# Bias strip and lambda products moved ahead of the first unit of a decoder trunk kernel

## The chip, the cores and the metric

The kernel runs on one core of one Trainium2 chip. The metric is the device time of one execution in microseconds (us); lower is better. The median of three runs stands for the kernel.

## The reference

The reference is a decoder trunk of two layers (sequence 256, width 2048). Only the first layer's mixer matters here:

```python
def parallel_mixer(h, w_in, w_out, rel_bias, lq1, lk1, lq2, lk2, subln, layer_idx):
    proj = jnp.einsum('bsd,de->bse', h, w_in)
    ...
    lam = (jnp.exp(jnp.sum(lq1 * lk1)) - jnp.exp(jnp.sum(lq2 * lk2)) + lam_init)
    a_out = diff_attention(aq, ak, av, rel_bias, lam, subln, lam_init)
    r_out = retention(rq, rk, rv, rg)
    mixed = jnp.concatenate([a_out, r_out], axis=-1)
    return jnp.einsum('bse,ed->bsd', mixed, w_out)
```

In `diff_attention` every softmax map gets a bias `rel_bias[bucket(distance)]`, and the second map of each head is subtracted with the weight `lam`. The rest of the trunk (a pooling mixer, two gated MLPs with a width-3 convolution, norms) is computed around it and is not touched.

## The kernel before

All weight matrices pass through the core in units of 512 x 512. SyncE (SP) loads a unit into one of four `raw` slots. ScalarE (ACT) rounds each of its four 128 x 512 tiles into `hi` (float32r), VectorE (DVE) writes the remainder `lo = raw - hi`, and TensorE (PE) multiplies with `hi` and `lo`. A pair of semaphores, `hi_done` and `lo_done`, counts the tiles, and `w_used` gives the single `hi`/`lo` buffer of each tile back.

The input projection has 56 units (14 groups of 4). The first four are done by `first_unit` (L640 to L655): per tile two products with `hi`, two with `lo`, and two with the low part of the activations (L645, L649, L653), each behind its own wait. These four units are loaded tile by tile, in the opening of the kernel. From unit 4 on, `token_unit` does the same in another order (L666, L671).

Two small things are prepared beside this stream. The *bias strip* is one product of `relb` (the relative bias, 32 x 8, and a row of ones) and `onehot` (33 x 384); ACT copies it out, writes it to memory and reads it back as a shifted pattern `bias`. *Lambda* begins with `lamp = lamv * lamv` on DVE (L1665), then a product with a matrix of ones on PE (L772), then an exponential on ACT (L1051) and two small steps on DVE. `strip_and_lambda` (L766 to L772) issues both products on PE. It is called behind unit 6 and behind the product `sum_squares` (L679) that adds up the squares of the first norm. The first reader of both results on PE is `scores` behind unit 12.

The data come by `CONSTS`, five small loads that SP issues behind its load for unit 4 (L474): `relb`, `onehot`, `lamv`, the identity and `sub`. All five count into one semaphore `c_in`; PE waits for it in `strip_and_lambda`, DVE behind unit 5 (L1664).

PE's program begins with a wait for the ones matrix (`setup`) and eight products of ones with ones into an unused bank (L776, `WARM_UP`); then the units come in the order of the text. Each float32 product stands as two passes in the trace. DVE's program begins with three memsets and a cast (L1609 to L1613) and goes on with `lo` of unit 0. GpSimd's program waits for the end of the kernel, where it multiplies a part of the last norm (L2013); it has no other work. Each engine runs its own list in order; nothing but the semaphores ties them.

Of the kernel before, what the change touches and what calls it, by code (L numbers as in the profile page):

```python
# [23 lines left out]
ALU = mybir.AluOpType  # L24
# [7 lines left out]
LAM_INIT = 0.8 - 0.6 * math.exp(-0.3 * 0)  # L32
POOL_WINDOWS = (2, 4, 8, 16)
RAW_SLOTS = 4
WARM_UP = 8
KT = 4


def trunk_kernel(nc, xT, rel_bias, norm_g, w_in, w_out, lam, subln, pool_w, pool_scale,
# [12 lines left out]
    NB = rel_bias.shape[0]  # L52
# [83 lines left out]
    with ctx:  # L136
        mixer = ExitStack()

        def sb(name, shape, dt=F32, stack=ctx):
            return stack.enter_context(nc.sbuf_tensor(name, shape, dt))  # L140
# [17 lines left out]
        ident = sb("ident", [P, P])  # L158

        with mixer:  # L160
# [19 lines left out]
            onehot = sb("onehot", [NB + 1, SPAN], stack=mixer)  # L180
            relb = sb("relb", [NB + 1, BD], stack=mixer)
            strip = sc[0:BD, 0, :]
            lamv = sb("lamv", [P, 4], stack=mixer)
            lamp = sb("lamp", [P, 4], stack=mixer)
            sub = sb("sub", [P, 2], stack=mixer)
# [3 lines left out]
            rden = sb("rden", [P, 4], stack=mixer)  # L189
        gate = bias  # L190
        am_blocks = mt[:, :, :].rearrange("p t s -> p (t s)")[:, 0:384]
        CONSTS = [(relb[0:NB, :], rel_bias), (onehot[:, :], bucket_onehot), (lamv[:, :], lam),
                  (ident[:, :], ident_in), (sub[:, :], subln)]
        TABLES = [(cos[:, :], rot_cos), (sin[:, :], rot_sin), (dec[:, :, :], decay), (pscale[:, :], pool_scale),
                  (pool_m[:, :, :], pool_matrix), (cw[:, :, :, :], conv)]
        N_CONST = len(CONSTS)
        N_TABLE = len(TABLES)
# [7 lines left out]
        def sem(name):  # L205
            return ctx.enter_context(nc.semaphore(name))
# [3 lines left out]
        w_tile = [sem(f"w_tile{i}") for i in range(12)]  # L210
        g_in = sem("g_in")
        c_in = sem("c_in")
        table_in = sem("table_in")
        raw_full = [sem(f"raw_full{i}") for i in range(RAW_SLOTS)]
        hi_done = sem("hi_done")
# [18 lines left out]
        lam_prod = sem("lam_prod")  # L234
# [109 lines left out]
        def acc_banks(i):  # L344

            return ps[:, 2 * (i % 2):2 * (i % 2) + 2, :]
# [35 lines left out]
        def _(sp):  # L382
# [55 lines left out]
            for n in range(U_OUT):  # L438
# [33 lines left out]
                if n == 4:  # L472
                    for dst, src in CONSTS:
                        sp.dma_start(dst, src).then_inc(c_in, 16)  # L474
# [66 lines left out]
        def _(pe):  # L541
# [133 lines left out]
            def sum_squares(n, bank):  # L675

                pe.wait_ge(sq_added, SQ_BASE[n + 1])
                if n != 2:
                    mm = pe.matmul(ps[:, bank, 0:S], ones[:, :], sqacc[:, 0, :], start=True, stop=True,  # L679
                                   skip_group_check=True)  # L680
                if n == 2:

                    for t in range(2):
                        mm = pe.matmul(ps[:, bank, S + t:S + t + 1], sqacc[:, 0, t * P:(t + 1) * P], ones[:, 0:1],
                                       start=t == 0, stop=True, skip_group_check=True)
                mm.then_inc(norm_sum, 1)
# [39 lines left out]
            def head_squares(n):  # L726

                if n == 0:
                    pe.wait_ge(ones_rounded, 1)
                pe.wait_ge(squares_lo, n + 1)  # L730
                if n:
                    pe.wait_ge(ssq_kept, n)
                pe.matmul(ps[:, 6, 0:S], ones_r[:, :], sq_hi[:, :], start=True, stop=False, skip_group_check=True)
                pe.matmul(ps[:, 6, 0:S], ones_r[:, :], sq_lo[:, :], start=False, stop=True,
                          skip_group_check=True).then_inc(ssq_mm, 1)
# [29 lines left out]

            def strip_and_lambda():  # L766

                pe.wait_ge(c_in, 16 * N_CONST)
                pe.wait_ge(setup, 3)
                pe.matmul(ps[0:BD, 4, 0:SPAN], relb[:, :], onehot[:, :], start=True, stop=True).then_inc(strip_mm, 1)  # L770
                pe.wait_ge(lam_prod, 1)
                pe.matmul(ps[:, 5, 0:2], ones[:, :], lamp[:, 0:2], start=True, stop=True).then_inc(lam_sum, 1)  # L772

            pe.wait_ge(setup, 1)
            for _ in range(WARM_UP):
                pe.matmul(ps[:, 7, 0:P], ones[:, :], ones[:, :], start=True, stop=True, skip_group_check=True)  # L776

            for n in range(U_OUT):
                G, j = divmod(n, 4)
                if n in ACC_AT:  # L780
                    i = ACC_AT[n]
                    if i >= 2 and ACCS[i - 2][0] in QUAD_GROUPS:
                        pe.wait_ge(rows_turned, QUAD_GROUPS.index(ACCS[i - 2][0]) + 1)
                    elif i == 2:
                        pe.wait_ge(first_turned, 1)
                    elif i > 2:
                        pe.wait_ge(evacuated, ACC_OUT[i - 2])

                def beside(kt, n=n):
                    for head, unit_n in enumerate(SQUARES_AT):  # L790
                        if (n, kt) == (unit_n, 1):
                            head_squares(head)

                if GROUPS[G][1] in "tq":
                    token_unit(n, acc_banks(i), j == 0, j == 3, j, beside)
                elif GROUPS[G][1] == "f":
                    half_unit(n, acc_banks(i), j % 2 == 0, j % 2 == 1, j % 2, beside)
                else:
                    first_unit(n, acc_banks(i))
                if n == 6:  # L800
                    sum_squares(0, 7)
                    strip_and_lambda()
                for a, at in enumerate(ATTN_START):
                    if n == at:
                        scores(a)
                    if n == at + 4:
                        attend(a)
                for r, at in enumerate(RET_START):
                    if n == at:
                        ret_scores(r)  # L810
                    if n == at + 1:
                        retain(r)
# [527 lines left out]
        def _(ve):  # L1340
# [270 lines left out]
            ve.memset(relb[NB:NB + 1, :], 1.0).then_inc(setup, 1)  # L1611
            ve.wait_ge(setup, 1)
            ve.tensor_copy(ones_r[:, :], ones[:, :]).then_inc(ones_rounded, 1)  # L1613
            for n in range(4):
                for kt in range(KT):
                    w_lo(n, 0, n, [kt])
                    h_lo_group(0, n, 0, [kt])
# [39 lines left out]
            for n in range(4, U_OUT):  # L1657
                w_lo(n, 0, n % 4, between=beside_lo(n))
                if n == 4:
                    turn_first_rows()  # L1660
                if n == 6:
                    fold_squares(0)
                if n == 5:
                    ve.wait_ge(c_in, 16 * N_CONST)  # L1664
                    ve.tensor_tensor(lamp[:, 0:2], lamv[:, 0:2], lamv[:, 2:4], ALU.mult).then_inc(lam_prod, 1)  # L1665
                    ve.tensor_scalar(sub[:, :], sub[:, :], 1.0 - LAM_INIT, None, ALU.mult).then_inc(setup, 1)
                if n == 46:
                    scale_quads(10)
                if n - 1 in ACC_END and n > 4:
                    if (n - 1) // 4 in QUAD_GROUPS:  # L1670
                        turn_rows((n - 1) // 4)
                    else:
                        take_out(ACC_END[n - 1])
                if n == 9:

                    ve.wait_ge(lam_exp, 1)
                    ve.tensor_tensor(lamv[:, 1:2], lamp[:, 3:4], lamp[:, 2:3], ALU.subtract).then_inc(lam_done, 1)
                    ve.wait_ge(lam_done, 1)
                    ve.tensor_scalar(lamv[:, 0:1], lamv[:, 1:2], -LAM_INIT, None, ALU.add).then_inc(lam_done, 1)
                for a, at in enumerate(ATTN_START):  # L1680
                    if n == at + 1:
                        softmax_front(a)
                    if n == at + 2:
                        softmax_back(a)
                        turn_maps(a)
                    if n == at + 5:
                        fold_head(a)
                for r, at in enumerate(RET_START):
                    if n == at + 1:
                        decay_scores(r)  # L1690
                    if n == at + 2:
                        fold_head(4 + r)
# [314 lines left out]
        @block.gpsimd  # L2007
        def _(pool_e):
            g_ = nc.gpsimd
            pool_e.wait_ge(weighted, 12)  # L2010
            for t in range(2):
                pool_e.wait_ge(rstd_copied, t + 1)
                g_.tensor_tensor(x[:, 8:12, token[t]], x[:, 8:12, token[t]],  # L2013
                                 rstd[:, token[t]].unsqueeze(1).to_broadcast([P, 4, P]), ALU.mult).then_inc(out_pool, 1)
# [82 lines left out]
```

## Time and profile before

| what | before |
|---|---|
| median of three runs | 1904.09 us (1903.6 to 1904.84) |
| the profiled execution | 1903.54 us |
| its span, first to last instruction | 1901.8 us |
| PE busy | 1893.7 us |
| DVE busy | 1415.2 us |
| ACT busy | 1065.3 us |
| GpSimd busy | 2.8 us |

The profiled execution took 1903.54 us, of which 1901.8 us are its span and 1.74 us lie around it; it is 0.55 us under the median. Times in the rows below count from the start of the span. A timeline row gives the start, the duration, the engine, the line and the operation with its tiles, and in brackets for how long the engine sat idle before it and what ended this. An engine name with a q (SPq, ACTq, POOLq) is the queue of that engine's sequencer, on which DMAs and other instructions without arithmetic stand; PEld is the loading of the stationary matrix.

### The profile page before, as it was taken

What the parts mean: (1) busy time and instruction counts of PE and PEld (TensorE: products, weight loads), DVE (VectorE), ACT (ScalarE), POOL (GpSimd) and SP (SyncE); (2) the same over time, 40 slices, a digit from 0 to 9 for tenths busy, and PEclk for the clock granted to TensorE, in tenths of its full rate; (3) what the DMA queues carried; (4) which work ended last, traced back from release to release, by engine and by line L of the source; (5) the groups of instructions that cost most, each with busy time, mean ns of one, the idle gap of its engine ahead of it and who ended that gap; (6) DMA issues with size and microseconds to landing.
All of it is one profiled execution on the core that took longest, in us unless ns stands there. A gap on an engine that the chain in (4) does not pass through costs nothing.

```text
span 1901.8 us, 26641 instructions
## 1 busy us (share of the span) xinstructions
PE 1893.7 (100%) x8570; PEld 1574.7 (83%) x8570; DVE 1415.2 (74%) x2329; ACT 1065.3 (56%) x1796; POOL 2.8 (0%) x6
## 2 busy tenths in 40 slices
PE   9999999999999999999999999999999999999998
PEld 7888888888888888888888888888888888888887
DVE  7767977777777777777766678777777777766665
ACT  7555545556555655556554556565555655555544
POOL 0000000000000000000000000000000000000000
PEclk9999999999999999999999999999999999999999
DMA  9876666666887777776665555677777777755653
GB/s 317 276 230 212 204 213 198 221 206 212 246 242 234 241 238 245 246 242 218 210 214 199 195 183 191 218 242 236 244 246 244 238 230 249 245 180 197 218 199 111
DMA packets 234384, 424.58 MB, mean 223 GB/s; under 512 B 14115, under 2 KB 54988, under 8 KB 234316
## 3 DMA queue, kind: packets, MB, share of 16 engines
q1 hardware_dynamic: 201484, 376.83, 61.6%
q10 hardware_dynamic: 32832, 46.86, 8.3%
q8 instruction: 41, 0.67, 0.1%
q14 instruction: 27, 0.22, 0.0%
HBM read 390.86 MB, written 31.21 MB: 222 GB/s over the span
## 4 chain that ended last, share of the span: by engine, by line
PE 100%; ACT 0%; DVE 0%; issue 0%
PE ps L666 61%; PE ps L671 30%; PE ps L552 2%; PE ps L556 1%; PE ps L630 1%; PE ps L645 0%; PE ps L649 0%; PE ps L634 0%; PE ps L653 0%; PE ps L595 0%; PE ps L597 0%; PE ps L596 0%; PE ps L776 0%; PE ps L841 0%; PE ps L843 0%; PE ps L747 0%
## 5 line engine op out<-in xcount | busy, mean ns | idle before, releaser
L915 ACT ACTIVATE hi<-raw 128x512 fp32r<-128x512 f32 x1336 | 831.9, 630 | 758.2 <-PE ps L671 710.9
L1345 DVE TENSOR_TENSOR lo<-raw,hi 128x512 fp32r<-128x512 f32 x1352 | 910.2, 689 | 449.2 <-ACT hi L915 437.1
L666 PE MATMUL ps<-hi,h 128*128 128x512 f32 x3648 | 977.7, 390 | 0.0
L666 PEld LDWEIGHTS ps<-hi,h 128*128 128x128 f32 x3648 | 682.7, 188 | 140.7
L671 PE MATMUL ps<-lo,h 128*128 128x512 f32 x1824 | 561.5, 389 | 0.0
L671 PEld LDWEIGHTS ps<-lo,h 128*128 128x128 f32 x1824 | 342.3, 188 | 71.5
L666 PE MATMUL ps<-hi,act 128*128 128x512 f32 x1296 | 346.4, 389 | 0.0
L666 PEld LDWEIGHTS ps<-hi,act 128*128 128x128 f32 x1296 | 243.2, 188 | 50.5
L671 PE MATMUL ps<-lo,act 128*128 128x512 f32 x648 | 199.5, 389 | 0.0
L671 PEld LDWEIGHTS ps<-lo,act 128*128 128x128 f32 x648 | 121.6, 188 | 25.2
L1120 ACT ACTIVATE yg<-u,cw 128x256 f32<-128x256 f32 x88 | 52.1, 592 | 18.8 <-DVE u L1774 18.8
L1120 ACT ACTIVATE yv<-u,cw 128x256 f32<-128x256 f32 x88 | 52.0, 591 | 14.8 <-DVE u L1774 14.8
L1774 DVE TENSOR_TENSOR u<-sqacc,rstd 128x512 f32<-128x512 f32 x84 | 54.1, 685 | 1.9 <-DMA sqacc<-turned_rows 1.9
L1763 DVE STREAM_TRANSPOSE sqt<-ps 128x1024 f32<-128x1024 f32 x42 | 52.2, 1243 | 0.0
L1809 DVE STREAM_TRANSPOSE u<-ps 32x256 f32<-32x256 f32 x96 | 42.8, 446 | 2.9
L552 PE MATMUL ps<-mixed,hi 128*128 128x512 f32 x128 | 43.9, 394 | 0.0
L1790 DVE SCALAR_TENSOR_TENSOR yg<-u,cw,yg 128x254 f32<-128x254 f32 x88 | 38.2, 477 | 0.0
L1782 DVE SCALAR_TENSOR_TENSOR yv<-u,cw,yv 128x255 f32<-128x255 f32 x88 | 36.6, 479 | 0.0
L1782 DVE SCALAR_TENSOR_TENSOR yg<-u,cw,yg 128x255 f32<-128x255 f32 x88 | 36.6, 479 | 0.0
L1790 DVE SCALAR_TENSOR_TENSOR yv<-u,cw,yv 128x254 f32<-128x254 f32 x88 | 36.5, 478 | 0.0
L666 PE MATMUL ps<-hi,mixed 128*128 128x512 f32 x128 | 34.2, 389 | 0.0
L556 PE MATMUL ps<-mixed,lo 128*128 128x256 f32 x128 | 34.2, 277 | 0.0
(208 smaller groups left out, 869.0 us busy)
## 6 DMA issues: line engine op xcount, KB each, us to landing
raw<-in_w_up SPq DMA_DIRECT2D x176, 1024.0 KB, 5.7
raw<-in_w_down SPq DMA_DIRECT2D x88, 1024.0 KB, 5.1
raw<-in_w_in SPq DMA_DIRECT2D x52, 1024.0 KB, 5.6
turned_rows<-sqt ACTq DMA_DIRECT2D x42, 512.0 KB, 5.9
sqacc<-turned_rows ACTq DMA_DIRECT2D x168, 128.0 KB, 6.0
raw<-in_w_out SPq DMA_DIRECT2D x16, 1024.0 KB, 6.0
raw<-in_w_in SPq DMA_DIRECT2D x16, 256.0 KB, 5.5
row_store<-sqt SPq DMA_DIRECT2D x8, 512.0 KB, 3.0
```

The source lines that it names most:

```text
L552: pe.matmul(ps[:, bank + m, :], hi[:, kt, m * P:(m + 1) * P], mv, start=first and kt == 0, stop=False, skip_group_check=True)
L556: return pe.matmul(ps[:, bank + m, S:2 * S], lo[:, kt, m * P:(m + 1) * P], mv[:, 0:S], start=False, stop=last and kt == KT - 1, skip_group ...
L666: pe.matmul(acc[:, t, :], xt, hi[:, kt, :], start=first and kt == 0 and half == 0, stop=False, skip_group_check=True)
L671: mm = pe.matmul(acc[:, t, :], xh, lo[:, kt, :], start=False, stop=last and kt == KT - 1, skip_group_check=True)
L915: a_.activation(out[:, kt, :], raw[:, slot, kt, :], ACT.Copy).then_inc(hi_done, 1)
L1120: a_.activation(y[:, m, :], u[:, m, :], ACT.Identity, scale=cw[:, l, bass.ds(t, 1), 2], bias=cw[:, l, bass.ds(t, 1), 3]).then_inc(y0, 1)
L1345: ve.tensor_tensor(halves[1][:, kt, :], raw[:, slot, kt, :], halves[0][:, kt, :].bitcast(F32), ALU.subtract).then_inc(lo_done, 1)
L1763: ve.transpose(turned_u.rearrange("p (q k s) -> p q k s", q=4, k=8), rows).then_inc(evacuated, 1)
L1774: scaled = ve.tensor_tensor(out, quads, r, ALU.mult)
L1782: ve.scalar_tensor_tensor(y[:, m, 1:S], u[:, m, 0:S - 1], cw[:, l, bass.ds(t, 1), 1], y[:, m, 1:S], ALU.mult, ALU.add).then_inc(y1, 1)
L1790: ve.scalar_tensor_tensor(y[:, m, 2:S], u[:, m, 0:S - 2], cw[:, l, bass.ds(t, 1), 0], y[:, m, 2:S], ALU.mult, ALU.add).then_inc(y2, 1)
L1809: ve.transpose(cols, rows).then_inc(x_turned, 1)
```

## The change

Three of the five small loads (`onehot`, `relb`, `lamv`) leave SP's list and stand first in GpSimd's, with a semaphore `early_in` of their own. DVE's product for lambda moves from behind unit 5 to ahead of `lo` of unit 0, behind a wait for `early_in`. The two products of `strip_and_lambda` move on PE from behind unit 6 to ahead of unit 0, behind a wait for `early_in`, and two of the eight products of ones are dropped.

```diff
-WARM_UP = 8
+WARM_UP = 6
...
-        CONSTS = [(relb[0:NB, :], rel_bias), (onehot[:, :], bucket_onehot), (lamv[:, :], lam),
-                  (ident[:, :], ident_in), (sub[:, :], subln)]
+        EARLY = [(onehot[:, :], bucket_onehot), (relb[0:NB, :], rel_bias), (lamv[:, :], lam)]
+        CONSTS = [(ident[:, :], ident_in), (sub[:, :], subln)]
...
+        early_in = sem("early_in")
...
             def strip_and_lambda():
-                pe.wait_ge(c_in, 16 * N_CONST)
+                pe.wait_ge(early_in, 16 * len(EARLY))
...
                 pe.matmul(ps[:, 7, 0:P], ones[:, :], ones[:, :], start=True, stop=True, skip_group_check=True)
+            strip_and_lambda()
...
                 if n == 6:
                     sum_squares(0, 7)
-                    strip_and_lambda()
...
             ve.tensor_copy(ones_r[:, :], ones[:, :]).then_inc(ones_rounded, 1)
+            ve.wait_ge(early_in, 16 * len(EARLY))
+            ve.tensor_tensor(lamp[:, 0:2], lamv[:, 0:2], lamv[:, 2:4], ALU.mult).then_inc(lam_prod, 1)
...
                 if n == 5:
                     ve.wait_ge(c_in, 16 * N_CONST)
-                    ve.tensor_tensor(lamp[:, 0:2], lamv[:, 0:2], lamv[:, 2:4], ALU.mult).then_inc(lam_prod, 1)
...
             g_ = nc.gpsimd
+            for dst, src in EARLY:
+                g_.dma_start(dst, src).then_inc(early_in, 16)
             pool_e.wait_ge(weighted, 12)
```

## Rows read from the trace of the kernel before

**Rows 1.** The page: busy time of each engine, and the chain that ended last.

```profile
PE 1893.7 (100%) x8570; PEld 1574.7 (83%) x8570; DVE 1415.2 (74%) x2329; ACT 1065.3 (56%) x1796; POOL 2.8 (0%) x6
...
PE 100%; ACT 0%; DVE 0%; issue 0%
```

**Rows 2.** Waits of PE over the whole span: total, times, longest.

```profile
PE ps L610 <- DVE rms L1980: 1.2, 1, 1.2
PE ps L776 <- DVE eps L1610: 1.1, 1, 1.1
```

**Rows 3.** Timeline, opening, PE and its weight loads.

```profile
1.06 3.78 PE L776 MATMUL ps<-ones 128*128 128x128 f32 x16 [1.06 <-DVE eps L1610]
...
4.93 0.46 PEld L645 LDWEIGHTS ps<-hi,h 128*128 128x128 f32 x2 [0.38 <-issue]
4.96 0.86 PE L645 MATMUL ps<-hi,h 128*128 128x512 f32 x2
...
7.16 0.30 PEld L649 LDWEIGHTS ps<-lo,h 128*128 128x128 f32 x2 [0.38 <-DVE lo L1345]
...
8.54 0.31 PEld L649 LDWEIGHTS ps<-lo,h 128*128 128x128 f32 x2 [0.15 <-DVE lo L1345]
```

**Rows 4.** Timeline, end of unit 3 and start of unit 4, PE alone.

```profile
24.57 0.62 PE L645 MATMUL ps<-hi,h 128*128 128x512 f32 x2
...
25.93 0.62 PE L645 MATMUL ps<-hi,h 128*128 128x512 f32 x2
...
27.29 1.07 PE L666 MATMUL ps<-hi,h 128*128 128x512 f32 x4
```

**Rows 5.** Chain that ended last, 40 to 48 us: start, us of the chain, what.

```profile
42.41 0.91 PE ps L666 x4
43.32 0.45 PE ps L671 x2
43.77 0.43 PE ps L679 x2
44.20 0.74 PE ps L770 x2
44.94 0.31 PE ps L772 x2
45.25 1.03 PE ps L666 x4
46.29 0.46 PE ps L671 x2
```

**Rows 6.** Timeline, opening, DMA issues, DVE and ACT.

```profile
0.75 0.43 ACTq L1005 DMA_DIRECT2D gains<-in_norm_g  x1
...
1.18 0.23 DVE L1613 CAST ones_r<-ones 128x128 fp32r<-128x128 f32 x1
...
1.21 0.44 ACTq L1006 DMA_DIRECT2D x<-in_xT  x1
...
1.69 1.28 ACT L1009 ACT_TABLE_LOAD   x1 [1.69 <-PEq L2087]
...
4.31 0.91 ACT L921 ACTIVATE h<-x,gains 128x256 fp32r<-128x256 f32 x2
4.41 0.69 DVE L1345 TENSOR_TENSOR lo<-raw,hi 128x512 fp32r<-128x512 f32 x1 [3.00 <-ACT hi L1018]
...
9.17 0.63 ACT L1018 ACTIVATE hi<-raw 128x512 fp32r<-128x512 f32 x1
...
11.90 0.69 DVE L1345 TENSOR_TENSOR lo<-raw,hi 128x512 fp32r<-128x512 f32 x1
```

**Rows 7.** Issues of the small loads on SP's queue (one line), and the next.

```profile
13.52 1.32 SPq L474 DMA_DIRECT2D relb<-in_rel_bias  x1
14.89 0.41 SPq L474 DMA_DIRECT2D onehot<-in_bucket_onehot  x1
15.34 0.36 SPq L474 DMA_DIRECT2D lamv<-in_lam  x1
...
16.69 0.43 SPq L387 DMA_DIRECT2D raw<-in_w_in  x1
```

**Rows 8.** DMA issues of 0 to 10 us: KB each, median us to landing.

```profile
x<-in_xT SPq DMA_DIRECT2D x7, 128.0 KB, 4.4
x<-in_xT SPq DMA_DIRECT2D x1, 512.0 KB, 5.9
x<-in_xT ACTq DMA_DIRECT2D x1, 128.0 KB, 3.2
gains<-in_norm_g ACTq DMA_DIRECT2D x1, 40.0 KB, 3.2
```

**Rows 9.** Lines 776, 719 and 645 by operation: ns min/median/max, first and last start.

```profile
L776 PE MATMUL ps<-ones x16: 421/421/581, 1.1 to 4.4; 128*128 128x128 f32 x16
...
L719 PE MATMUL ps<-amT,v x16: 270/274/275, 101.0 to 192.3; 128*128 128x128 f32 x16
...
L645 PE MATMUL ps<-hi,h x32: 387/389/632, 5.0 to 26.2; 128*128 128x512 f32 x32
```

**Rows 10.** Busy time by stretch: PE, PEld, DVE, ACT, POOL, PEclk (granted clock), DMA share, GB/s.

```profile
4.00:5.00 1.00, 0.88 (x5) 0.62 (x4) 0.59 (x1) 1.00 (x3) 0.00 (x0) 1.00 0.98 310
...
10.00:30.00 20.00, 20.00 (x89) 16.53 (x89) 16.30 (x30) 14.94 (x28) 0.00 (x0) 1.00 1.06 376
```

**Rows 11.** GpSimd's line 2013 by operation: ns min/median/max, first and last start.

```profile
L2013 POOLq MODIFY_POOL_CONFIG  x2: 11/11/11, 0.8 to 0.8; - x2
L2013 POOL TENSOR_TENSOR x<-x,rstd x2: 1267/1277/1287, 1888.0 to 1895.5; 128x512 f32<-128x512 f32 x2
```

**Rows 12.** DVE's product for lambda, from the instructions of tile lamp.

```profile
L1665 DVE TENSOR_TENSOR lamp<-lamv x1: 154/154/154, 34.7 to 34.7; 128x2 f32<-128x2 f32 x1
```

## The prediction

> **What bounds the kernel now.** I read the page first: PE is busy for 1893.7 of 1901.8 us, the chain that ended last is PE from end to end, and no other engine is over 1415.2 us [rows 1]. Then PE's waits: over the whole span there are only two that the profile counts, 1.1 us before the first product of ones and 1.2 us in the last norm [rows 2]. Between them PE goes from one product to the next. So time is won or lost in two ways only: PE gets fewer products (or faster ones), or its first unit starts earlier or later. What DVE, ACT and the weight loads do matters as far as it reaches the start of PE's stream. That the DMA engines are full from 10 to 30 us (share 1.06) costs PE nothing, for it is busy for all 20.00 us there [rows 10].
>
> The opening needs the timeline. PE runs the products of ones from 1.06 to 4.84 us, and unit 0 starts at 4.96 [rows 3], when ACT has `hi` and, from 4.31 us on, the first `h` [rows 6]. The first steps lose a little more: two waits for `lo`, 0.38 and 0.15 us [rows 3], and a slow first product (below). From there a tile takes 1.36 us (25.93 - 24.57) and unit 4 starts at 27.29 [rows 4]. Counted back over 16 tiles, 27.29 - 16 x 1.36 = 5.53 us: the stream runs as if it had started at 5.53 at its steady pace. This is the mark that the changed kernel has to meet.
>
> **The change part by part.** *Products behind unit 6.* In the chain the strip takes 0.74 us, lambda 0.31, and the four products behind them 1.03 instead of 0.91, for the stream restarts: 0.74 + 0.31 + 0.12 = 1.17 us [rows 5]. They go from there, and since nothing but PE is late behind them, all 1.17 us come off the end.
>
> *Two products of ones fewer.* Six take 6/8 of 3.78 = 2.83 us and end at 3.89 instead of 4.84 [rows 3]. This gains nothing by itself, since the data of unit 0 are there only at about 4.8 to 4.9 us [rows 6]. It makes room for 0.95 us.
>
> *Products ahead of unit 0.* They cost the same 1.17 us, but only from the time E at which all three early loads have landed. DVE's product for lambda (0.154 us, [rows 12]) runs beside the strip on PE. So the steady start moves to E + 1.17, and against before the balance is (E + 1.17 - 5.53) - 1.17 = E - 5.53: with PE at one pace, the change wins when the loads land before 5.53 us and loses when they land later. Everything hangs on E.
>
> *E.* The trace of before shows no DMA on GpSimd's queue, so I bound it. From below by ACT's queue, a second queue in the same moments: issues at 0.75 and 1.21, so 0.46 us apart [rows 6], each landing in 3.2 us [rows 8]. Three of them would land by 0.75 + 2 x 0.46 + 3.2 = 4.87 us. From above by the slowest issue of the same loads, `relb` on SP's queue with 1.37 us to the next (14.89 - 13.52, [rows 7]), and SP's landing of 4.4 us [rows 8]: 0.75 + 2 x 1.37 + 4.4 = 7.89 us. I take 5.6 us, a quarter of the way, because ACT's queue is the nearer row: the same microsecond and small loads beside SP's stream. The balance is then +0.1 us, between -0.7 and +2.4.
>
> The Trainium skill, "DMA: Bandwidth & Descriptors", section "Anatomy of one DMA — SWDGE (gpsimd) path", gives a DMA issued by GpSimd a fixed 2.0 us and its bytes at 436 GB/s; if three followed each other wholly, an estimate from that page would be 6.9 us for E and the balance +1.4. It speaks against the change; no run here shows the pace of that queue.
>
> *The clock.* The granted clock reads 1.00, the upper level (2.4 GHz), in the stretches of the opening [rows 10], but the durations say otherwise: a pass of 128 columns lasts 421 ns among the products of ones and 274 ns later, and the first pass of unit 0 lasts 632 ns against 389 [rows 9]. So PE runs at the lower level (1.2 GHz) from 1.06 to about 5.3 us, 4.3 us of unbroken work, and at the upper one from there. In the changed kernel PE stands idle from 3.89 to E. The strip and lambda may then run wholly at the lower level, and their 1.05 us of passes take at most 1.05 us more. I take somewhat over half of it, +0.6.
>
> *What DVE's wait holds up.* Behind it stand `lo` of unit 0 and all later ones; before, that first `lo` starts at 4.41 [rows 6]. With E = 5.6 it ends at about 5.6 + 0.15 + 0.69 = 6.45, still ahead of PE's need at about 7. ACT needs PE's first release for unit 1 at 9.17 and SP needs DVE's only from unit 4 on; with PE later by some 1.2 us both have slack. Nothing added.
>
> *Three loads off SP's queue.* Their issues go from 13.52 to 15.70 [rows 7]. The load of unit 5 stands behind them and can be issued about 2.2 us before 16.69: it waits only for `lo` of unit 1, which is done at about 12.6 [rows 6]. Its issue is earlier; PE has no wait there, so the gain is nothing. The 0.154 us taken out behind unit 5 on DVE are nothing either, since DVE waits for ACT.
>
> *The sum.* -1.17 + (5.6 + 1.17 - 5.53) + 0.6 = +0.7 us against the profiled execution, 1903.54 + 0.7 = 1904.2. That execution is 0.55 us under the median of 1904.09, so in terms of the median 1904.8. Own range of this case: -0.7 to 2.4 + 1.05 = +3.5, or 1903.4 to 1907.6.
>
> **The rivals.** *Hidden whole.* If the loads land by 3.8 us, the two products take the room of the dropped ones, unit 0 starts at 4.96 as before, and the kernel is 1.17 us faster: 1902.9. For it: a single early load can land by 0.75 + 3.2 = 3.95. Against it: there are three on one queue.
>
> *The clock starts again.* If the idle time makes the rise count anew from E, the first 4.3 us of work from there run at half pace and lose 2.2 us instead of 0.6: +0.1 + 2.2 = +2.3, 1906.4. For it: the rise came after 4.3 us of unbroken work in before. Against it: the pause is only 1.7 us.
>
> *The loads stand behind something on GpSimd (the other side).* GpSimd's queue carries two instructions MODIFY_POOL_CONFIG at 0.8 us that belong to line 2013, a multiplication that runs at 1888.0 [rows 11]. So they have been placed ahead of that line's waits, right where the early loads will stand, and what they start is not shown: 11 ns each on the queue. If they stand ahead of the loads and hold them, E moves by that time. The nearest row of an engine taking in tables is ACT's, 1.28 us [rows 6]; twice this gives E = 5.6 + 2.6 = 8.2, with 2.2 us for the clock a balance of +4.9: 1909.0. From E = 7.2 with the slow clock, or 9.3 without it, the loss passes 3.8 us. Against it: the pair belongs to a later line and may well stay behind the loads. The Trainium skill, "GPSIMD Engine Reference", section "Instruction dispatch", states that the first call to a freshly loaded kernel costs some 6 us more; by an estimate from that page E is 11.6 and the time about 1912. No row here shows such a load.
>
> **How the numbers follow.** Forecast 0.53, hidden whole 0.08, clock again 0.15, loads held 0.22, and 0.02 for a gain that no row shows. 0.2% of the kernel is 3.8 us, about what a measurement can tell from no change. The forecast, hidden whole and clock again all lie inside that, and so does 0.04 of the loads held: same 0.80. Slower is the rest of the loads held, 0.18; faster 0.02, since the products removed are worth 1.17 us at most. The range runs from 1902.9 (hidden whole) to 1909.0 (loads held by the nearest row) and leaves out the worse part of that rival, some 0.12.
>
> **What would show it.** In the changed trace: no L770 and L772 near 44 us, and 1.17 us between `sum_squares` and the next unit gone; six products of ones ending at 3.9; the start of the strip on PE, which is E, at 5 to 8 us; unit 4 starting E - 5.53 + 1.17 us (and the clock's part) later than 27.29; the first passes of unit 0 at 632 or at 389 ns. If the issue of the three loads on GpSimd starts well after 0.8 us, or the strip after 9, the loads were held and the forecast is wrong. If unit 0 starts by 5.0, all was hidden. A new wait of PE between 27 and 1890 us would speak against the whole way of counting.

## The result and the profile after

| what | before | after |
|---|---|---|
| median of 22 runs each | 1904.05 us (1903.6 to 1904.99) | 1907.26 us (1905.82 to 1909.44) |
| ratio to before | | 1.0016 (95% interval 1.0010 to 1.0022) |
| the profiled execution | 1903.54 us | 1909.44 us |
| its span | 1901.8 us | 1907.6 us |
| PE busy | 1893.7 us | 1896.1 us |

The change makes the kernel 3.2 us slower, 0.16%. That is inside the 0.2% called "same" in the prediction, and the interval is clear of no change. The runs of after lie further apart (3.6 us) than those of before (1.4 us), and the profiled execution is the slowest of them, so its 5.8 us of extra span are more than the 3.2 us of the medians.

The chain that ended last, in its first 16 us, tells the new opening (start, us of the chain, what):

```profile
1.27 0.71 POOL onehot L2013
1.99 0.51 POOL relb L2013
2.50 3.94 DMA lamv<-in_lam
6.44 0.04 issue
6.48 1.45 PE ps L771 x2
7.93 0.52 PE ps L773 x2
8.44 1.06 PE ps L646 x2
9.50 0.85 PE ps L650 x2
...
13.77 0.63 PE ps L646 x2
14.40 0.46 PE ps L650 x2
```

Before, this chain was PE alone. Now it begins on GpSimd: three issues, one behind the other, then the landing of the last load, and only then PE. The two lines L771 and L773 are the strip and lambda. Together they take 1.97 us here; behind unit 6 they took 1.05 [rows 5]. The passes of unit 0 take 0.85 us a pair and, from about 14 us on, 0.46. Unit 4 starts at 32.85 us (timeline, PE alone):

```profile
32.85 1.07 PE L667 MATMUL ps<-hi,h 128*128 128x512 f32 x4
```

The queue of GpSimd in the timeline, and the landings of its loads in the DMA issues of 0 to 12 us (KB, us to landing):

```profile
1.27 0.71 POOL L2013 DMA_DIRECT2D onehot<-in_bucket_onehot  x1 [0.82 <-POOLq L2091]
1.98 0.53 POOL L2013 DMA_DIRECT2D relb<-in_rel_bias  x1
2.50 0.57 POOL L2013 DMA_DIRECT2D lamv<-in_lam  x1
```

```profile
onehot<-in_bucket_onehot POOLq DMA_DIRECT2D x1, 49.5 KB, 3.7
relb<-in_rel_bias POOLq DMA_DIRECT2D x1, 1.0 KB, 3.5
lamv<-in_lam POOLq DMA_DIRECT2D x1, 2.0 KB, 3.9
```

So E, the time of the last landing, is 2.50 + 3.94 = 6.44 us. PE's waits and, by operation, lines 771, 773 and 646 (ns min/median/max, first and last start) answer to [rows 2, 9]:

```profile
PE ps L771 <- DMA lamv<-in_lam: 2.5, 1, 2.5
PE ps L611 <- DVE rms L1982: 1.2, 1, 1.2
PE ps L672 <- DVE lo L1346: 1.1, 1, 1.1
PE ps L777 <- DVE eps L1611: 1.1, 1, 1.1
```

```profile
L771 PE MATMUL ps<-onehot,relb x2: 806/825/844, 6.5 to 7.1; 33*8 33x384 f32 x2
L773 PE MATMUL ps<-lamp,ones x2: 352/362/372, 7.9 to 8.1; 128*128 128x2 f32 x2
...
L646 PE MATMUL ps<-hi,h x32: 389/389/774, 8.3 to 31.7; 128*128 128x512 f32 x32
```

PE waits 2.5 us for the loads, and what follows runs at the lower level of its clock (1.2 GHz): the first passes of unit 0 last up to 774 ns, against 389 later. The granted clock reads 1.00 there, so this is a reading of the durations; the run with later loads below shows passes of the same length where the granted clock reads 0.50.

Behind unit 6, the chain of 46 to 54 us shows what was won; the lines stand where [rows 5] stood:

```profile
49.33 0.43 PE ps L680 x2
49.76 0.93 PE ps L667 x4
50.69 0.46 PE ps L672 x2
```

From `sum_squares` on, the chain reaches the next L672 in 1.36 us in place of 2.52 (46.29 - 43.77): 1.16 us less.

The sum of the profiled execution: unit 4 starts at 32.85 us in place of 27.29 [rows 4], 5.56 us later; 1.16 come back behind unit 6; and the third wait above, near 1153 us, takes 1.49 us from one product to the next in place of 0.23, where DVE had sat 2.5 us waiting for a transfer that landed late. 5.56 - 1.16 + 1.26 = 5.7 of the 5.8 us. I do not count that last wait to the change: it stands in no profile of the experiments below in which both products are ahead of unit 0, and a shorter one for the same transfer (1.67 us on DVE, 0.26 us on PE) stands in the run with lambda alone moved. Why that transfer was late in this execution is not known.

### The profile page after: what moved, and what is told of

It is laid out like the page before. It is cut to its first block, busy times and chain, and to the rows that moved or that the text cites. A ratio compares the mean times of both kernels' runs of the same rounds, so it can differ in the third digit from the quotient of the medians.

```text
span 1907.6 us, 26633 instructions
## 1 busy us (share of the span) xinstructions
PE 1896.1 (99%) x8566; PEld 1576.1 (83%) x8566; DVE 1415.0 (74%) x2329; ACT 1063.9 (56%) x1796; POOL 4.5 (0%) x9
## 4 chain that ended last, share of the span: by engine, by line
PE 99%; DVE 0%; DMA 0%; issue 0%; ACT 0%; POOL 0%; DVEq 0%; POOLq 0%
PE ps L667 60%; PE ps L672 30%; PE ps L553 2%; PE ps L557 1%; PE ps L631 1%; PE ps L646 0%; PE ps L654 0%; PE ps L650 0%; PE ps L635 0%; PE ps L596 0%; PE ps L598 0%; PE ps L597 0%; DMA lamv<-in_lam 0%; PE ps L842 0%; PE ps L844 0%; PE ps L748 0%
## 5 line engine op out<-in xcount | busy, mean ns | idle before, releaser
L672 PE MATMUL ps<-lo,h 128*128 128x512 f32 x1824 | 561.7, 389 | 1.1 <-DVE lo L1346 1.1
L672 PEld LDWEIGHTS ps<-lo,h 128*128 128x128 f32 x1824 | 342.3, 188 | 72.9 <-DVE lo L1346 1.5
L672 PE MATMUL ps<-lo,act 128*128 128x512 f32 x648 | 199.4, 389 | 0.0
L672 PEld LDWEIGHTS ps<-lo,act 128*128 128x128 f32 x648 | 121.6, 188 | 25.3
```

The source lines that it names most:

```text
L672: mm = pe.matmul(acc[:, t, :], xh, lo[:, kt, :], start=False, stop=last and kt == KT - 1, skip_group_check=True)
```

## The experiments

The theory: with PE at one pace the change costs E - 5.53, so 6.44 - 5.53 = 0.9 us; the other 2.3 us come from the clock, which rises late because PE pauses from 4.00 to 6.48 us. The rivals: the pause is innocent, and the loads, GpSimd's queue, DVE's wait or the place of the products cost the time. "Before" is 1904.05 us for the first four and 1903.81 us for the last four, which were measured on another occasion. Eleven runs each.

**No pause.** The changed kernel with more products of ones:

```diff
-WARM_UP = 6
+WARM_UP = 14
```

> The changed kernel with 14 products of ones in place of 6, so that PE has work until the early loads land. Theory (late loads plus a clock that is not raised because PE pauses): the loads land at 6.4 to 6.5 us as in the changed kernel's trace, the clock rises near 5.3 us as before the change, and only E - 5.53 = about 0.9 us is left: 1905.0 us (1904.6 to 1905.4). Rival (the pause is innocent, the loss of 3.2 us comes from the loads, GpSimd's queue or the held DVE): 1907.3 us or more, for none of that is changed.

1904.79 us (1904.02 to 1906.08), ratio 1.0003 (0.9994 to 1.0012): 0.74 us over before, which by the interval could be nothing, and 2.47 under the changed kernel with 6. PE in its timeline:

```profile
1.07 5.79 PE L777 MATMUL ps<-ones 128*128 128x128 f32 x28 [1.07 <-DVE eps L1611]
6.79 0.81 PE L771 MATMUL ps<-onehot,relb 33*8 33x384 f32 x2
7.52 0.38 PE L773 MATMUL ps<-lamp,ones 128*128 128x2 f32 x2
7.77 0.72 PE L646 MATMUL ps<-hi,h 128*128 128x512 f32 x2
...
29.67 1.07 PE L667 MATMUL ps<-hi,h 128*128 128x512 f32 x4
```

The same loads, the same held DVE, the same order; only the pause is gone, and the strip takes 0.81 us in place of 1.45. The strip starts at 6.79 behind the last product of ones, a little after E. By the balance unit 4 should start at 27.29 + 6.79 + 1.17 - 5.53 = 29.72 us; it starts at 29.67. This execution (1905.64) is 0.85 us above the median: 0.9 us of its extra span come far behind the opening, about half of that at one wait for ACT near 1245 us.

**The pause alone.** The kernel before with fewer products of ones:

```diff
-WARM_UP = 8
+WARM_UP = 3
```

> The kernel before with 3 products of ones in place of 8 and nothing else, so that PE pauses from about 2.5 us to unit 0 at 4.96, as long as it pauses in the changed kernel (2.5 us). Theory: the clock rises later, unit 0 runs its first tiles at the lower level, and the time goes up by 1 to 4 us, 1906.3 us as the middle, with a wider spread from run to run than before (0.7 us). Rival (a pause is innocent): 1904.05 us, spread as before.

1905.88 us (1904.62 to 1908.78), ratio 1.0010 (1.0001 to 1.0019): 1.83 us slower with five products less. Its profiled execution, with 1904.79 us, is one of the lower ones:

```profile
1.06 1.65 PE L776 MATMUL ps<-ones 128*128 128x128 f32 x6 [1.06 <-DVE eps L1610]
5.12 1.19 PE L645 MATMUL ps<-hi,h 128*128 128x512 f32 x2 [2.40 <-ACT h L921]
6.11 1.05 PE L649 MATMUL ps<-lo,h 128*128 128x512 f32 x2
6.96 1.05 PE L653 MATMUL ps<-hi,h 128*128 128x512 f32 x2
7.81 0.90 PE L645 MATMUL ps<-hi,h 128*128 128x512 f32 x2
8.55 0.62 PE L649 MATMUL ps<-lo,h 128*128 128x512 f32 x2
```

Unit 0 starts 0.16 us later than before and stays at the lower level until about 8.4 us instead of 5.3. A pause of PE costs by itself about what the changed kernel lost beyond E, though the interval of the 1.83 us runs from 0.2 to 3.6. The wider spread is not shown: the 4.2 us come from one run, the other ten lie within 2.2 us, like the 33 runs of before that belong to them.

**The loads alone.** The kernel before, with the loads on GpSimd and all their users in the old places:

```diff
-        CONSTS = [(relb[0:NB, :], rel_bias), (onehot[:, :], bucket_onehot), (lamv[:, :], lam),
-                  (ident[:, :], ident_in), (sub[:, :], subln)]
+        EARLY = [(onehot[:, :], bucket_onehot), (relb[0:NB, :], rel_bias), (lamv[:, :], lam)]
+        CONSTS = [(ident[:, :], ident_in), (sub[:, :], subln)]
...
+            for dst, src in EARLY:
+                g_.dma_start(dst, src).then_inc(early_in, 16)
```

> The kernel before with the three loads issued by GpSimd at its start; both products and DVE's product stay behind units 6 and 5, with 8 products of ones. Theory: the loads are hidden, 1904.05 us (1903.8 to 1904.4), and the load of unit 5 is issued about 2 us earlier without any use. Rival (GpSimd's queue or the loads themselves disturb the opening or the end): 1905 to 1907.3 us.

1903.95 us (1903.27 to 1905.21), ratio 1.0000 (0.9991 to 1.0009). GpSimd's queue and the loads cost nothing that can be measured, and that three issues leave SP's queue gains nothing. The load of unit 5 is issued at 15.56 us, 1.1 us earlier than before [rows 7] and not 2.

**The products behind unit 0.** The changed kernel with 8 products of ones, and:

```diff
-            strip_and_lambda()
...
+                if n == 0:
+                    strip_and_lambda()
```

DVE's product moves behind its own work of unit 0 in the same way.

> The changed kernel with 8 products of ones, the two products behind unit 0 in place of ahead of it, and DVE's product behind its work of unit 0. By then (about 11 us) the loads have landed and the clock is up. Theory: PE's stream is full, so the products cost the same 1.17 us there as behind unit 6: 1904.05 us (1903.8 to 1904.5). Rival (taking them away from unit 6 is itself worth something, or being early costs something besides the wait): a difference of 1 us or more either way.

1904.08 us (1903.4 to 1905.32), ratio 1.0000 (0.9991 to 1.0009). PE in its timeline:

```profile
10.85 0.81 PE L771 MATMUL ps<-onehot,relb 33*8 33x384 f32 x2
...
28.25 1.07 PE L667 MATMUL ps<-hi,h 128*128 128x512 f32 x4
```

The strip starts at 10.85 us, all loads have landed and the clock is up, and unit 4 starts at 28.25, 0.96 later than before. What comes off behind unit 6 goes on behind unit 0: in a full stream the place of these products is worth nothing that the medians show.

**Earlier loads.** Two of the three loads on ACT's queue, and 9 products of ones:

```diff
-WARM_UP = 6
+WARM_UP = 9
...
+            sc_e.dma_start(EARLY[2][0], EARLY[2][1]).then_inc(act_in, 16)
             sc_e.dma_start(gains[:, :, :], norm_g).then_inc(g_in, 16)
+            sc_e.dma_start(EARLY[1][0], EARLY[1][1]).then_inc(act_in, 16)
...
-            for dst, src in EARLY:
+            for dst, src in EARLY[0:1]:
```

> The changed kernel with its three loads on two queues: onehot first on GpSimd, lamv and relb on ACT's queue as first and third issue (the gains and a tile of x go behind them by 0.46 and 0.92 us), and 9 products of ones. By the rows of the changed kernel and of before the last load lands at about 5.0 us, the products of ones end at 5.3, so PE does not pause. Theory (balance E - 5.53, no pause): with E taken as 5.3 a balance of -0.2 us, 1903.85 us (1903.5 to 1904.5). Rival (early products are slow in themselves, whenever the loads come): 1905 us or more.

1904.94 us (1903.79 to 1908.15), ratio 1.0008 (0.9999 to 1.0017). A miss in the median, though the interval just includes no change. The runs fall apart: five lie between 1903.79 and 1904.45, where they were expected, and the upper five between 1905.61 and 1908.15. The profiled execution is one of the first group (1904.06):

```profile
5.59 0.16 DVE L1620 TENSOR_TENSOR lamp<-lamv 128x2 f32<-128x2 f32 x1 [4.18 <-DMA relb<-in_rel_bias]
5.66 0.80 PE L773 MATMUL ps<-onehot,relb 33*8 33x384 f32 x2 [0.38 <-issue]
...
7.07 0.51 ACT L924 ACTIVATE h<-x,gains 128x256 fp32r<-128x256 f32 x1 [2.01 <-DMA x<-in_xT]
```

E is 5.6, not 5.0, since `relb` took 3.9 us to land, so PE still pauses for a short while after the ninth product. The strip's passes are at the upper level all the same (0.80 us, as without a pause). And the tile of x that was put behind the loads lands later and holds ACT for 2.01 us: unit 4 starts at 28.98 where the balance says 27.29 + 5.66 + 1.17 - 5.53 = 28.59. That the upper group are runs with a late clock fits their size, but of those no profile was taken.

**Lambda first.** The kernel before with only lambda's product moved; `lamv` is the first issue on ACT's queue:

```diff
-WARM_UP = 8
+WARM_UP = 7
...
+            sc_e.dma_start(lamv[:, :], lam).then_inc(early_in, 16)
             sc_e.dma_start(gains[:, :, :], norm_g).then_inc(g_in, 16)
...
+            pe.wait_ge(lam_prod, 1)
+            pe.matmul(ps[:, 5, 0:2], ones[:, :], lamp[:, 0:2], start=True, stop=True).then_inc(lam_sum, 1)
```

> The kernel before with lambda's product alone moved: lamv is the first issue on ACT's queue (the gains and a tile of x 0.46 us later), DVE's product stands ahead of unit 0, PE's lambda product stands behind 7 products of ones, which end at 4.4 us; the strip stays behind unit 6. By the rows lamv lands at 0.75 + 3.2 = 3.95 us, so the product runs before unit 0's data are there. Theory: E is below 5.53 and the 0.31 us of lambda come off: 1903.75 us (1903.5 to 1904.1). Rival (the gains are needed at 4.3 us and land 0.46 us later, which gives it back): 1904.05 us or up to 0.5 us more.

1904.92 us (1904.47 to 1905.76), ratio 1.0006 (0.9996 to 1.0015); a miss. The interval includes no change, but every run lies above the median of before. The load and the product were in time, but something else was not:

```profile
4.13 0.36 PE L778 MATMUL ps<-lamp,ones 128*128 128x2 f32 x2
...
4.93 0.70 PE L646 MATMUL ps<-hi,h 128*128 128x512 f32 x2 [0.44 <-ACT h L923]
...
6.40 0.51 ACT L923 ACTIVATE h<-x,gains 128x256 fp32r<-128x256 f32 x1 [1.61 <-DMA x<-in_xT]
...
7.48 0.73 PE L646 MATMUL ps<-hi,h 128*128 128x512 f32 x2 [0.92 <-ACT hi L1021]
```

Unit 0 starts at 4.93 with lambda done, as the theory wants. Then the second tile is late by 0.92 us: its x is issued 0.48 us later than before and lands after 4.7 us instead of 3.2 [rows 8], so ACT waits 1.61 us for it. The gains, which the rival named, were in time. Unit 4 starts at 28.29 us, 1.00 later than before, and behind unit 6 only 0.23 us come off in place of 0.31: the strip stays, and the products behind it still restart.

**Later loads.** The changed kernel with two more loads ahead on GpSimd, and 19 products of ones:

```diff
-WARM_UP = 6
+WARM_UP = 19
-        EARLY = [(onehot[:, :], bucket_onehot), (relb[0:NB, :], rel_bias), (lamv[:, :], lam)]
-        CONSTS = [(ident[:, :], ident_in), (sub[:, :], subln)]
+        EARLY = [(ident[:, :], ident_in), (sub[:, :], subln),
+                 (onehot[:, :], bucket_onehot), (relb[0:NB, :], rel_bias), (lamv[:, :], lam)]
+        CONSTS = []
...
```

> The changed kernel with two more loads (the identity and sub) ahead of the three on GpSimd, so that the last is issued some 1.2 us later, and 19 products of ones, so that PE has work until about 7.7 us. Theory (balance E - 5.53, no pause): E about 7.7, balance +2.2 us, 1906.2 us (1905.8 to 1906.9); against the run with 14 products of ones that is the 1.2 us of E and nothing else. Rival (later loads are hidden by the slack of the opening): 1904.8 us as with the three loads.

1907.25 us (1906.34 to 1909.16), ratio 1.0017 (1.0008 to 1.0026). Nothing is hidden by slack, so the rival falls; but the size was wrong. In the profiled execution (1908.71, one of the slowest) the last load is issued 1.05 us later and then takes 5.5 us to land instead of 3.9, so E is 9.1 and the balance 9.1 - 5.53 = 3.6 us. That the median, too, is 3.4 over before proves nothing about E, for this execution lies 1.5 us above the median and lost time to the clock besides. PE ran out of products of ones at 7.0. This profile shows the clock itself; busy time by stretch, then the granted clock, DMA share, GB/s, and two rows of PE's timeline:

```profile
4.00:7.00 3.00, 3.00 (x26) 2.85 (x25) 0.00 (x0) 1.93 (x5) 0.12 (x1) 1.00 0.95 287
7.00:9.00 2.00, 0.04 (x1) 0.00 (x0) 0.00 (x0) 1.51 (x4) 0.00 (x0) 1.00 1.06 377
9.00:11.00 2.00, 1.88 (x8) 1.10 (x9) 1.90 (x5) 0.93 (x2) 0.00 (x0) 1.00 1.07 377
11.00:14.00 3.00, 3.00 (x9) 2.31 (x8) 3.00 (x7) 1.03 (x2) 0.00 (x0) 0.50 1.08 365
14.00:17.00 3.00, 3.00 (x13) 2.45 (x13) 1.50 (x4) 1.86 (x4) 0.00 (x0) 0.93 1.06 376
```

```profile
12.05 1.05 PE L647 MATMUL ps<-hi,h 128*128 128x512 f32 x2
...
33.59 1.07 PE L668 MATMUL ps<-hi,h 128*128 128x512 f32 x4
```

PE works until 7, is idle from 7 to 9 (busy 0.04 of 2.00), works again from 9, and the granted clock falls to 0.50 only from 11 on, when PE has been at work again for about 2 us; it is back soon after 14. The pair at 12.05 takes 1.05 us where the granted clock reads 0.50, as long as the pairs of unit 0 in the run with the pause alone; that ties those durations to the lower level. Unit 4 starts 1.54 us later than the balance says (33.59 against 27.29 + 9.12 + 1.17 - 5.53 = 32.05), about half of the 3.4 us at the lower level.

**A shorter pause.** The changed kernel with 9 products of ones:

```diff
-WARM_UP = 6
+WARM_UP = 9
```

> The changed kernel with 9 products of ones in place of 6: PE's pause before the strip falls from 2.5 to about 1.1 us, E stays 6.45. Theory (a pause keeps the clock at its lower level or not by its length and place): between the 1904.8 us without a pause and the 1907.3 us with one of 2.5 us, 1905.5 us as the middle, with runs at both ends. Rival (any pause costs the same): 1907.3 us.

1907.49 us (1904.43 to 1907.93), ratio 1.0013 (1.0004 to 1.0022). The median is the rival's, but the runs lie at both ends, as the theory has it: five between 1904.43 and 1906.2, six between 1907.49 and 1907.93. PE's pause in the profile is 1.26 us. The profiled execution (1907.7) is of the upper group:

```profile
PE ps L771 <- DMA lamv<-in_lam: 1.3, 1, 1.3
```

```profile
L771 PE MATMUL ps<-onehot,relb x2: 806/825/844, 6.5 to 7.1; 33*8 33x384 f32 x2
```

```profile
32.61 1.07 PE L667 MATMUL ps<-hi,h 128*128 128x512 f32 x4
```

Here too the strip runs at 825 ns a pass, as in the changed kernel, and unit 4 starts at 32.61, 3.1 us over the balance (29.47). So even a pause of 1.26 us right after the products of ones can cost what one of 2.5 us costs; in other executions of the same kernel it costs next to nothing, for the two lowest lie 0.6 us over before, less than the 0.9 of E alone. The run with earlier loads also had nine products of ones, with a pause of 0.38 us behind them, and its strip was at the upper level; these are one profiled execution each.

None of these kernels is faster than the one before.

## Why the prediction was right and where it was not

*The range and the direction* held: 1907.26 is inside 1902.9 to 1909.0, and it is within the 3.8 us called "same". But the forecast's own case, 1904.8, was 2.5 us too low. That 1907.26 also lies inside that case's own range, 1903.4 to 1907.6, is luck: its top is made of a very late E (7.89) and 1.05 us for the clock, and the runs showed an E of 6.44 and some 2.5 us for the clock. The top of the whole range, 1909.0, was set by a rival that did not come. Nearest to what came is the rival named "the clock starts again", forecast at 1906.4 with a chance of 0.15: its 2.2 us for the clock and the measured E make 3.1 of the 3.2 us. Its kind is shown, its working is not: it let the lower level last for 4.3 us from E, but the profiled execution shows it from 6.48 to about 14 us, the run with the pause alone from 5.12 to about 8.4, and the run with later loads not until PE had been at work again for about 2 us.

*What bounds the kernel* and *the balance E - 5.53* held. Unit 4 of the run without a pause starts within 0.05 us of it, and products moved within a full stream change nothing (1904.08). The removal behind unit 6 was put at 1.17 us and measured 1.16.

*E* was mis-sized: 5.6 us forecast, 6.44 measured, inside the bounds of 4.87 to 7.89. I took ACT's queue as the nearer row. GpSimd's first issue stands at 1.27 us, not at 0.75 as ACT's [rows 6], its issues take 0.71 and 0.53 in place of 0.46, and the last load lands after 3.9 us in place of 3.2. The term is 0.84 us short. The Trainium skill, "DMA: Bandwidth & Descriptors", section "Anatomy of one DMA — SWDGE (gpsimd) path", gives a fixed 2.0 us to such a DMA; here each load takes 3.5 to 3.9 us from its issue to its landing, and the three overlap. That the estimate from that page for wholly serial loads, 6.9, came out near 6.44 is chance: the two errors go opposite ways.

*The clock* is the step that failed. I took 0.6 us, as if only the strip and lambda could run at the lower level, and argued against the rival that a pause of 1.7 us is short. The measured pause is 2.5 us, and removing it gives back 2.47 us: not only the strip and lambda but the first tiles of unit 0 run at the lower level. In the profiled execution PE is at the lower level from 6.48 to about 14 us, which makes unit 4 start 3.4 us over the balance (32.85 against 27.29 + 6.48 + 1.17 - 5.53 = 29.41). With the measured terms, 0.9 for E and 2.5 for the pause make 3.4, against 3.2 measured; how long the lower level lasted in the median run is not shown.

*DVE's wait* was rightly put at nothing: the run without a pause holds DVE just as long, and its unit 4 starts where the balance says. *The loads off SP's queue* were too (1903.95 with the loads alone), though on a wrong reading: the `lo` that is done at about 12.6 is the third of unit 1's four, the last is done at 13.66, and the load of unit 5 came 1.1 us earlier, not 2.2.

*Loads held on GpSimd*, the rival of the other side with 0.22, did not come. The two instructions stand behind the loads now, in the instructions of line 2017:

```profile
L2017 POOLq MODIFY_POOL_CONFIG  x2: 37/37/37, 3.1 to 3.1; - x2
```

*Hidden whole* did not come either, and could not: at the lower level the strip and lambda take 1.97 us, so the loads would have to land by about 3.0, before any early load in these traces does.

What stays open: what decides, in a kernel with a pause, whether an execution ends in the lower or in the upper group. When the clock rose is known only for the profiled executions, and there its moment differs although PE is at work from 1.06 us on in each (but for 0.12 us in before): the passes become fast at about 4.0 us (lambda first), 4.2 (later loads), 5.3 (before) and 6.1 (no pause). The products of ones of the runs with 14 and with 19 of them show it in their medians:

```profile
L777 PE MATMUL ps<-ones x28: 274/421/582, 1.1 to 6.6; 128*128 128x128 f32 x28
L778 PE MATMUL ps<-ones x38: 274/275/581, 1.1 to 6.8; 128*128 128x128 f32 x38
```

So the 4.3 us of work that the prediction took from the trace of before are no constant. A pause that begins within this spread, like the one from 5.28 us in the run with the shorter pause, may come before the rise or behind it; that this makes the two groups is an argument and not shown.

## What to carry to other kernels

Work that is moved to the front of a stream that is full from then on gains only if its data are there before the stream could have started; compare the landing of the last load with that moment before moving it. Filler that keeps PE at work until the first real unit should last until that unit starts: here filler that ended 2.5 us too early cost 2.47 us, twice the 1.17 us that the moved products take. A small DMA put ahead of another on the same queue is not free in the opening, for the one behind it may land much later than its issue moved.

## What the runs showed that was not expected

- The granted clock in the rows reads 1.00 in the openings of before and after, although the passes last far longer there (825 against 484 ns for the strip, 774 against 389 in unit 0 of after); only a fall during the run shows as 0.50. In an opening the durations tell the level, not that column.
- A pause of PE of 2.5 us costs 1.8 to 2.5 us after it has ended. The runs of the kernels with a pause lie 2.8 to 4.4 us apart, those of before 1.4 to 2.8. The Trainium skill, "TensorE: Matmul & The Clock Gate", section "HAM oscillation — how this bites in real kernels", says that idle gaps of PE let the clock fall, and the gaps of its example are longer than any here. The run with later loads agrees that the clock falls after an idle gap, here of 2.1 us, and adds that the fall can come when PE has been busy again for about 2 us. In the changed kernel the clock does not fall but has not yet risen when the pause begins at 4.00 us: every pass of its products of ones lasts 421 ns or more.
- A 128 KB tile of x on ACT's queue lands 3.2 us after an issue at 1.21, but 4.7 us after one at 1.69 and 4.9 after one at 2.17. Some 0.5 us of delay in the issue became 2 us in the landing. A fifth small load on GpSimd's queue lands after 5.5 us, where `lamv` as the third does after 3.5 to 4.4.
